# Laying the low products of a weight unit one for one between the high products of the next

## The chip, the cores and the metric

The kernel runs on one core of a Trainium2 chip. The metric is the time of one execution on the device in microseconds (us). Five engines work side by side, each through its own list of instructions in order, and wait for one another by semaphores: TensorE (PE; its weight loads are shown apart as PEld), VectorE (DVE), ScalarE (ACT), GpSimd (POOL, unused here) and SyncE (SP), which issues the transfers from memory.

## The reference

Two layers over 256 latent tokens of width 2048, with 256 context tokens that feed the first layer. All in fp32. Nearly all of the arithmetic is products of the tokens with large weight matrices:

```python
def reference(...):
    for i in range(DEPTH):                                   # 2 layers
        mod = (c_act @ mod_w[i] + mod_b[i])[:, None, :]
        sh1, sc1, g1, sh2, sc2, g2 = jnp.split(mod, N_MOD, axis=-1)
        h_lat = modulate(rms_norm(x, norm_mix_g[i]), sh1, sc1)
...
        if is_attn:                                          # layer 0
            y_lat, y_ctx = attention_mixer(h_lat, h_ctx, ...)
        else:                                                # layer 1
            y_lat = hyena_mixer(h_lat, ...)
        x = x + g1 * y_lat
        x = x + g2 * sq_relu_mlp(modulate(rms_norm(x, norm_mlp_g[i]), sh2, sc2), mlp_w1[i], mlp_w2[i])
    return rms_norm(x, final_g)
```

`sq_relu_mlp(h, w1, w2)` is `square(relu(h @ w1)) @ w2` with w1 2048 x 8192 and w2 8192 x 2048, so the two MLPs hold most of the weights.

## The kernel before

**Splitting.** To keep fp32 accuracy with a rounded matmul format (fp32r), each operand is a sum of a high part (rounded) and a low part (what the rounding left). Weights arrive in *units* of 512 x 256 values: `raw[:, n % 4]`, a ring of four slots. ScalarE copies the unit to the high part (`act_split`, writes `w_hi`), VectorE subtracts it from the raw values to get the low part (`dve_split`, writes `w_lo`); both rings have four slots too. The tokens lie as `lat` or `alt`, 512 columns per block of 128 features: 256 columns of high parts, then 256 of low parts.

**The products of a unit** (`pe_unit`). For each of 4 blocks of features (`kk`) and 2 halves of 128 output columns (`fb`) there is a *high product* (line 371: the weights' high part against all 512 columns) and a *low product* (line 380: the weights' low part against the 256 columns of high tokens, added to the same PSUM bank). The 8 high products of a unit come first, then its 8 low products. In the key projection the context tokens go along, which makes 16 and 16. In the value projection (`pe_values`, lines 408 and 415) tokens and weights change roles, and high and low products both stream 512 columns.

**Groups of units.** Eight units make a group (`pe_iter`): units 0 to 3 run through all 16 feature blocks for output columns in banks 0 and 1, units 4 to 7 for those in banks 2 and 3. A group has a number T; the MLP of each layer has 32 of them, in four quarters, each with 4 groups of the first product (tokens in `lat`) and 4 of the second (tokens in `alt`). In the attention layer, 32 units are woven between the steps of the softmax by a table, and the first group of Hyena's output projection has an order of its own; both call `pe_unit` directly. In the Hyena layer `before(n)` puts products of the convolution ahead of unit n.

**Who waits for whom.** TensorE waits for `hi_ready` (the copy) before the high products of a unit, for `split_ready` (the subtraction) before its low products, for the tokens (`ready`), and for `psum_free` before units 0 and 4. Its last low product of a unit signals `units_done`. ScalarE's copy into a slot waits for the unit's landing and for `units_done` of the unit that used the slot four units ago; VectorE's subtraction waits for the copy alone. SyncE issues the transfer of unit n + 4 when unit n is subtracted (`split_ready`), and between those, in the same list, the *slabs* of the modulation weights, which VectorE multiplies and adds up behind its subtractions. The read-outs of the PSUM banks (`act_head`, `dve_head` and their tails) stand in the lists of ScalarE and VectorE behind certain splits, and wait for `units_done` too.

Of the kernel before, what the change touches and what calls it, by code (L numbers as in the profile page):

```python
# [25 lines left out]
P = 128  # L26
# [101 lines left out]
def build(nc, a):  # L128
# [9 lines left out]
    with stack:  # L138
# [92 lines left out]
        unit_landed = [sem(f"unit_landed{j}") for j in range(RING)]  # L231
        slab_landed = [sem(f"slab_landed{j}") for j in range(RING)]
        hi_ready, split_ready = sem("hi_ready"), sem("split_ready")
        units_done = sem("units_done")
        lo_copied, psum_free = sem("lo_copied"), sem("psum_free")
        slabs_used, acc_ready = sem("slabs_used"), sem("acc_ready")
        start_landed = [sem(f"start_landed{j}") for j in range(START_RING)]
# [117 lines left out]
        def pe_unit(e, T, n, g, j, tile, ready=None, ctx_tile=None):  # L355

            e.wait_ge(hi_ready, 8 * T + n + 1)
            if ready:

                e.wait_ge(ready[0], ready[1])  # L360
            if j == 0:

                e.wait_ge(psum_free, 2 * T + g - 1)
            for kk in range(UNIT_KB):
                kb = j * UNIT_KB + kk
                if ready and len(ready) == 3 and kk == 2:
                    e.wait_ge(ready[0], ready[2])
                for fb in range(2):
                    for t, bank in ((tile, 2 * g + fb), (ctx_tile, 4 + 2 * g + fb)):
                        if t is not None:  # L370
                            e.matmul(ps[:, bank, :], w_hi[:, n % RING, kk, fb * P:(fb + 1) * P], t[:, kb, :],  # L371
                                     start=(kb == 0), stop=False)

            e.wait_ge(split_ready, 8 * T + n + 1)
            for kk in range(UNIT_KB):
                kb = j * UNIT_KB + kk
                for fb in range(2):
                    for t, bank in ((tile, 2 * g + fb), (ctx_tile, 4 + 2 * g + fb)):
                        if t is not None:
                            mm = e.matmul(ps[:, bank, 0:TOK], w_lo[:, n % RING, kk, fb * P:(fb + 1) * P],  # L380
                                          t[:, kb, 0:TOK], start=False, stop=(kb == KB - 1))
            mm.then_inc(units_done, 1)

        def pe_iter(e, T, tile, ready, ctx_tile=None, stats=None, before=None):

            for n in range(8):
                if before:
                    before(n)
                if stats is not None and n == 7:
                    pe_stats(e, *stats)  # L390
                pe_unit(e, T, n, n // 4, n % 4, tile, ready(n % 4), ctx_tile)

        V_BANKS = (0, 1, 4, 5)

        def pe_values(e, T, after_unit):

            for n in range(8):
# [5 lines left out]
                for kk in range(2):  # L403
                    kb = 2 * n + kk
                    for part in range(2):
                        for tb, bank in enumerate(V_BANKS):
                            act = (lat, alt)[tb // 2][:, kb, ds(part * TOK + tb % 2 * P, P)]
                            e.matmul(ps[:, bank, :], act, hi[:, kk, :], start=(kb == 0 and part == 0), stop=False)

                e.wait_ge(split_ready, 8 * T + n + 1)  # L410
                for kk in range(2):
# [36 lines left out]
        def act_split(e, T, n):  # L448
            e.wait_ge(unit_landed[n % RING], 16 * (2 * T + n // 4 - 1))

            e.wait_ge(units_done, 8 * T + n - 3)
            e.activation(w_hi[:, n % RING], raw[:, n % RING], ACT.Copy).then_inc(hi_ready, 1)  # L452

        def dve_split(e, T, n):
            e.wait_ge(hi_ready, 8 * T + n + 1)
            e.tensor_tensor(w_lo[:, n % RING], raw[:, n % RING], w_hi[:, n % RING].bitcast(F32),  # L456
                            ALU.subtract).then_inc(split_ready, 1)

# [656 lines left out]
        @block.tensor  # L1115
        def _(e):
            e.sem_inc(units_done, 8)
            e.sem_inc(taps_mm, 4)

            e.sem_inc(mod_cols, 1)  # L1120
# [950 lines left out]
```

## Time and profile before

| | us |
|---|---|
| median of the runs | 2599.7 |
| lowest and highest run | 2599.48, 2600.33 |
| span of the profiled execution | 2601.3 |
| TensorE, matmuls busy | 2461.9 (95%) |
| TensorE, weight loads busy | 2070.6 (80%) |
| VectorE busy | 1951.6 (75%) |
| ScalarE busy | 1170.5 (45%) |

The profile is one execution, and the span runs from its first to its last instruction. A row of the timeline has the start of an instruction, or of a row of like instructions behind one another, and the time from the start of the first to the end of the last. Matmuls overlap: a row's time is longer than the distance to the next row's start, so paces are read from starts. The mean granted TensorE clock is 0.971 of full speed over the span.

### The profile page before, as it was taken

How to read it: one execution, taken by the hardware profiler on the slowest of the kernel's cores; microseconds unless marked ns; L12 is line 12 of the kernel's file. 1: busy time of each engine (PE TensorE's matmuls, PEld its weight loads, DVE VectorE, ACT ScalarE, POOL GpSimd, SP SyncE). 2: the span in 40 equal slices, each digit the busy share in tenths (PEclk: the TensorE clock that was granted, in tenths of full speed). 3: DMA queues.
4: the chain of work that ended last, by engine and by line, in shares of the span. 5: the costliest groups of instructions: out<-in, count | busy, mean ns of one | idle time of the engine just before them, and what ended most of it. 6: DMA issues, size and time to landing. Idle time of an engine off the chain costs nothing.

```text
span 2601.3 us, 39595 instructions
## 1 busy us (share of the span) xinstructions
PE 2461.9 (95%) x13332; PEld 2070.6 (80%) x13332; DVE 1951.6 (75%) x2352; ACT 1170.5 (45%) x1611; POOL 0.2 (0%) x4
## 2 busy tenths in 40 slices
PE   6879998888999999999998999999899999999998
PEld 2248876777788888888887888888778888888887
DVE  6767777688988877877888889878786565555665
ACT  2235256535444444444446444434534444444444
POOL 0000000000000000000000000000000000000000
PEclk9989998898999999999998999999899999999999
DMA  8856865476988888888786655647696665665653
GB/s 311 299 205 229 290 189 180 150 272 236 323 307 276 289 283 281 278 273 278 270 273 236 235 197 194 235 162 239 213 341 212 189 187 187 188 190 185 188 189 124
DMA packets 441211, 610.37 MB, mean 235 GB/s; under 512 B 18875, under 2 KB 383644, under 8 KB 439068
## 3 DMA queue, kind: packets, MB, share of 16 engines
q1 hardware_dynamic: 439676, 599.98, 69.3%
q10 hardware_dynamic: 1440, 9.18, 1.0%
q8 instruction: 54, 0.88, 0.1%
q14 instruction: 41, 0.34, 0.0%
HBM read 596.50 MB, written 10.49 MB: 233 GB/s over the span
## 4 chain that ended last, share of the span: by engine, by line
PE 75%; DVE 9%; ACT 6%; issue 5%; DMA 5%; SPq 1%; DVEq 0%; ACTq 0%
PE ps L371 43%; PE ps L380 22%; DMA raw<-in_mlp_w 3%; PE ps L1139 2%; DVE w_lo L456 2%; PE ps L1371 2%; DVE acc L468 2%; ACT w_hi L452 2%; ACT hm L900 1%; PE ps L1361 1%; DVE sm L1803 1%; DMA raw<-in_attn_w_out 1%; PE ps L1156 1%; PE ps L442 1%; PE ps L1175 1%
## 5 line engine op out<-in xcount | busy, mean ns | idle before, releaser
L452 ACT ACTIVATE w_hi<-raw 128x1024 fp32r<-128x1024 f32 x720 | 761.5, 1060 | 1088.1 <-PE ps L380 857.9
L456 DVE TENSOR_TENSOR w_lo<-raw,w_hi 128x1024 fp32r<-128x1024 f32 x720 | 877.8, 1223 | 465.6 <-ACT w_hi L452 462.0
L371 PE MATMUL ps<-lat,w_hi 128*128 128x512 f32 x3136 | 817.3, 400 | 35.8 <-ACT w_hi L452 16.4
L371 PEld LDWEIGHTS ps<-lat,w_hi 128*128 128x128 f32 x3136 | 572.3, 191 | 148.4 <-issue 33.4
L371 PE MATMUL ps<-alt,w_hi 128*128 128x512 f32 x2624 | 675.0, 396 | 10.4 <-DVE alt L1790 6.2
L371 PEld LDWEIGHTS ps<-alt,w_hi 128*128 128x128 f32 x2624 | 476.0, 190 | 97.5 <-issue 6.6
L380 PEld LDWEIGHTS ps<-lat,w_lo 128*128 128x128 f32 x3136 | 433.7, 191 | 31.8 <-DVE w_lo L456 0.4
L380 PE MATMUL ps<-lat,w_lo 128*128 128x256 f32 x3136 | 446.1, 283 | 0.0
L380 PEld LDWEIGHTS ps<-alt,w_lo 128*128 128x128 f32 x2624 | 362.6, 191 | 28.4 <-DVE w_lo L456 2.7
L468 DVE SCALAR_TENSOR_TENSOR acc<-slab,silu,acc 128x1024 f32<-128x1024 f32 x300 | 378.6, 1279 | 8.0 <-DMA slab<-in_mod_w 7.0
L380 PE MATMUL ps<-alt,w_lo 128*128 128x256 f32 x2624 | 373.7, 283 | 1.9 <-DVE w_lo L456 1.9
L588 DVE SCALAR_TENSOR_TENSOR x<-ps,mod,x 128x256 f32 (+1 forms) x160 | 69.6, 476 | 18.7 <-ACT lo_sum L578 18.3
L1427 ACT ACTIVATE spec<-ps 128x512 f32<-128x512 f32 x32 | 18.1, 590 | 112.4 <-PE ps L1175 112.4
L578 ACT ACTIVATE lo_sum<-ps,mod 128x256 f32<-128x256 f32 x144 | 59.1, 461 | 12.2 <-PE ps L380 12.2
L1371 PE MATMUL ps<-back,y_spec 128*128 128x256 f32 x256 | 57.7, 379 | 0.0
L593 DVE TENSOR_TENSOR x<-x,lo_sum 128x512 f32 (+1 forms) x80 | 55.4, 692 | 2.8
L1488 ACT ACTIVATE probs<-ps,sm,rs_q 128x512 f32<-128x512 f32 x32 | 24.9, 778 | 62.3 <-DVE sm L1806 62.3
L1371 PEld LDWEIGHTS ps<-back,y_spec 128*128 128x128 f32 x256 | 47.5, 190 | 5.9
L1139 PE MATMUL ps<-slab,silu 128*2 128x512 f32 x64 | 37.9, 724 | 12.2 <-DVE start_part L1716 8.5
L612 DVE SCALAR_TENSOR_TENSOR sum_sb<-sum_sb 128x512 f32<-128x512 f32 x64 | 44.3, 692 | 2.2
L617 ACT ACTIVATE alt<-sum_sb 128x512 f32 (+1 forms) x64 | 40.2, 628 | 10.0 <-DVE sum_sb L612 10.0
L610 DVE TENSOR_TENSOR sum_sb<-ps,lo_sum 128x512 f32<-128x512 f32 x64 | 43.7, 684 | 0.4
(191 smaller groups left out, 1495.5 us busy)
## 6 DMA issues: line engine op xcount, KB each, us to landing
raw<-in_mlp_w SPq DMA_DIRECT2D x512, 512.0 KB, 3.8
slab<-in_mod_w SPq DMA_DIRECT2D x352, 512.0 KB, 6.0
raw<-in_hy_w_in SPq DMA_DIRECT2D x96, 512.0 KB, 4.4
raw<-in_attn_w_in SPq DMA_DIRECT2D x48, 512.0 KB, 4.6
raw<-in_mod_w SPq DMA_DIRECT2D x32, 512.0 KB, 6.9
raw<-in_attn_w_out SPq DMA_DIRECT2D x32, 512.0 KB, 4.6
raw<-in_hy_w_out SPq DMA_DIRECT2D x32, 512.0 KB, 5.8
spec_dram<-spec ACTq DMA_DIRECT2D x8, 1024.0 KB, 7.3
```

The source lines that it names most:

```text
L371: e.matmul(ps[:, bank, :], w_hi[:, n % RING, kk, fb * P:(fb + 1) * P], t[:, kb, :], start=(kb == 0), stop=False)
L380: mm = e.matmul(ps[:, bank, 0:TOK], w_lo[:, n % RING, kk, fb * P:(fb + 1) * P], t[:, kb, 0:TOK], start=False, stop=(kb == KB - 1))
L452: e.activation(w_hi[:, n % RING], raw[:, n % RING], ACT.Copy).then_inc(hi_ready, 1)
L456: e.tensor_tensor(w_lo[:, n % RING], raw[:, n % RING], w_hi[:, n % RING].bitcast(F32), ALU.subtract).then_inc(split_ready, 1)
L468: e.scalar_tensor_tensor(acc[:, ac], slab[:, slot], scale, acc[:, ac], ALU.mult, ALU.add).then_inc(slabs_used, 1)
L578: ins = e.activation(lo_sum[:, g, fb], ps[:, 2 * g + fb, TOK:2 * TOK], ACT.Identity, bias=bias, scale=mod[:, ds(self.gate + f, 1)])
L588: ins = e.scalar_tensor_tensor(xf, ps[:, 2 * g + fb:2 * g + fb + 1, 0:TOK], mod[:, ds(self.gate + f, 1)], xf, ALU.mult, ALU.add)
L593: e.tensor_tensor(xg, xg, lo_sum[:, g], ALU.add).then_inc(psum_free, 1)
L610: e.tensor_tensor(sum_sb[:, g], self.bank(g, 0), lo_sum[:, g], ALU.add).then_inc(psum_free, 1)
L612: e.scalar_tensor_tensor(sum_sb[:, g], sum_sb[:, g], 0.0, sum_sb[:, g], ALU.max, ALU.mult).then_inc(squared, 1)
L1139: mm = e.matmul(ps[0:2, 4 + b, :], pair, start_slot(j)[:, b * 512:(b + 1) * 512], start=(r == 0), stop=(r == len(PE_SLABS) - 1))
L1371: mm = e.matmul(ps[:, 4 + 2 * hf, fb * TOK:(fb + 1) * TOK], y_spec[:, hf, f, fb * P:(fb + 1) * P], back[:, f, :], start=(f == 0), stop=(f ...
```

## The change

The order inside a group changes (`pe_iter`). It now runs over nine blocks: block 0 holds the 8 high products of unit 0, block n the high products of unit n with the low products of unit n - 1 between them, one for one, and block 8 the low products of unit 7. A high product and the low product behind it add to the same bank (except in block 4, where the banks change). All waits of a block stand at its head, apart from that for the second half of the tokens. `pe_unit` and `pe_values` keep their order.

There are two signals now: `hi_done` from the last high product of a unit, `units_done` from its last low product. ScalarE's copy waits for `hi_done` of the unit four before; VectorE's subtraction, which overwrites the low part, waits for `units_done` of that unit in addition to the copy.

```diff
--- before.py
+++ after.py
@@ -231,7 +231,7 @@
         unit_landed = [sem(f"unit_landed{j}") for j in range(RING)]
         slab_landed = [sem(f"slab_landed{j}") for j in range(RING)]
         hi_ready, split_ready = sem("hi_ready"), sem("split_ready")
-        units_done = sem("units_done")
+        units_done, hi_done = sem("units_done"), sem("hi_done")
         lo_copied, psum_free = sem("lo_copied"), sem("psum_free")
         slabs_used, acc_ready = sem("slabs_used"), sem("acc_ready")
         start_landed = [sem(f"start_landed{j}") for j in range(START_RING)]
@@ -368,8 +368,9 @@
                 for fb in range(2):
                     for t, bank in ((tile, 2 * g + fb), (ctx_tile, 4 + 2 * g + fb)):
                         if t is not None:
-                            e.matmul(ps[:, bank, :], w_hi[:, n % RING, kk, fb * P:(fb + 1) * P], t[:, kb, :],
-                                     start=(kb == 0), stop=False)
+                            mm = e.matmul(ps[:, bank, :], w_hi[:, n % RING, kk, fb * P:(fb + 1) * P], t[:, kb, :],
+                                          start=(kb == 0), stop=False)
+            mm.then_inc(hi_done, 1)
 
             e.wait_ge(split_ready, 8 * T + n + 1)
             for kk in range(UNIT_KB):
@@ -381,14 +382,52 @@
                                           t[:, kb, 0:TOK], start=False, stop=(kb == KB - 1))
             mm.then_inc(units_done, 1)
 
+        def pe_high(e, n, kk, fb, tile, ctx_tile):
+            kb = n % 4 * UNIT_KB + kk
+            for t, bank in ((tile, n // 4 * 2 + fb), (ctx_tile, 4 + n // 4 * 2 + fb)):
+                if t is not None:
+                    mm = e.matmul(ps[:, bank, :], w_hi[:, n % RING, kk, fb * P:(fb + 1) * P], t[:, kb, :],
+                                  start=(kb == 0), stop=False)
+            return mm
+
+        def pe_low(e, n, kk, fb, tile, ctx_tile):
+            kb = n % 4 * UNIT_KB + kk
+            for t, bank in ((tile, n // 4 * 2 + fb), (ctx_tile, 4 + n // 4 * 2 + fb)):
+                if t is not None:
+                    mm = e.matmul(ps[:, bank, 0:TOK], w_lo[:, n % RING, kk, fb * P:(fb + 1) * P], t[:, kb, 0:TOK],
+                                  start=False, stop=(kb == KB - 1))
+            return mm
+
         def pe_iter(e, T, tile, ready, ctx_tile=None, stats=None, before=None):
 
-            for n in range(8):
-                if before:
-                    before(n)
-                if stats is not None and n == 7:
-                    pe_stats(e, *stats)
-                pe_unit(e, T, n, n // 4, n % 4, tile, ready(n % 4), ctx_tile)
+
+            for n in range(9):
+                if n < 8:
+                    if before:
+                        before(n)
+                    if stats is not None and n == 7:
+                        pe_stats(e, *stats)
+                    ready_n = ready(n % 4)
+                    e.wait_ge(hi_ready, 8 * T + n + 1)
+                    e.wait_ge(ready_n[0], ready_n[1])
+                    if n % 4 == 0:
+
+                        e.wait_ge(psum_free, 2 * T + n // 4 - 1)
+                if n > 0:
+
+                    e.wait_ge(split_ready, 8 * T + n)
+                for kk in range(UNIT_KB):
+                    if n < 8 and kk == 2 and len(ready_n) == 3:
+                        e.wait_ge(ready_n[0], ready_n[2])
+                    for fb in range(2):
+                        if n < 8:
+                            hi = pe_high(e, n, kk, fb, tile, ctx_tile)
+                        if n > 0:
+                            lo = pe_low(e, n - 1, kk, fb, tile, ctx_tile)
+                if n < 8:
+                    hi.then_inc(hi_done, 1)
+                if n > 0:
+                    lo.then_inc(units_done, 1)
 
         V_BANKS = (0, 1, 4, 5)
 
@@ -405,7 +444,8 @@
                     for part in range(2):
                         for tb, bank in enumerate(V_BANKS):
                             act = (lat, alt)[tb // 2][:, kb, ds(part * TOK + tb % 2 * P, P)]
-                            e.matmul(ps[:, bank, :], act, hi[:, kk, :], start=(kb == 0 and part == 0), stop=False)
+                            mm = e.matmul(ps[:, bank, :], act, hi[:, kk, :], start=(kb == 0 and part == 0), stop=False)
+                mm.then_inc(hi_done, 1)
 
                 e.wait_ge(split_ready, 8 * T + n + 1)
                 for kk in range(2):
@@ -448,11 +488,13 @@
         def act_split(e, T, n):
             e.wait_ge(unit_landed[n % RING], 16 * (2 * T + n // 4 - 1))
 
-            e.wait_ge(units_done, 8 * T + n - 3)
+            e.wait_ge(hi_done, 8 * T + n - 3)
             e.activation(w_hi[:, n % RING], raw[:, n % RING], ACT.Copy).then_inc(hi_ready, 1)
 
         def dve_split(e, T, n):
             e.wait_ge(hi_ready, 8 * T + n + 1)
+
+            e.wait_ge(units_done, 8 * T + n - 3)
             e.tensor_tensor(w_lo[:, n % RING], raw[:, n % RING], w_hi[:, n % RING].bitcast(F32),
                             ALU.subtract).then_inc(split_ready, 1)
 
@@ -1115,6 +1157,7 @@
         @block.tensor
         def _(e):
             e.sem_inc(units_done, 8)
+            e.sem_inc(hi_done, 8)
             e.sem_inc(taps_mm, 4)
 
             e.sem_inc(mod_cols, 1)
```

On TensorE, in the loop over the last groups of the second MLP (`w_hi`, `w_lo` the weights' parts, `alt` the tokens, `ps` the banks), unit 7 stood so before, as every unit did:

```order
L357 REGISTER_ALU
L371 MATMUL ps<-alt,w_hi 128x512 [waits hidden_ready,hi_ready]
L371 MATMUL ps<-alt,w_hi 128x512 x7
L380 MATMUL ps<-alt,w_lo 128x256 [waits split_ready]
L380 MATMUL ps<-alt,w_lo 128x256 x7
```

The same loop now, its blocks 0 and 1 (the pairs of a block go on to eight):

```order
L415 ISA [waits hidden_ready,hi_ready]
L389 MATMUL ps<-alt,w_hi 128x512 [waits psum_free]
L389 MATMUL ps<-alt,w_hi 128x512 x7
L411 REGISTER_ALU
L389 MATMUL ps<-alt,w_hi 128x512 [waits split_ready,hidden_ready,hi_ready]
L397 MATMUL ps<-alt,w_lo 128x256
L389 MATMUL ps<-alt,w_hi 128x512
```

The low products have moved one unit back, and the wait for the subtraction stands ahead of the next unit's first high product.

On VectorE, in the last of these groups, the last subtraction and the read-out of the first two banks behind it stood so:

```order
L456 TENSOR_TENSOR w_lo<-raw,w_hi 128x1024 [waits hi_ready]
L584 ISA
L588 ISA [waits lo_copied]
L588 REGISTER_ALU
L588 SCALAR_TENSOR_TENSOR x<-ps,mod,x 128x256
```

and now:

```order
L498 TENSOR_TENSOR w_lo<-raw,w_hi 128x1024 [waits units_done,hi_ready]
L626 ISA
L630 ISA [waits lo_copied]
L630 REGISTER_ALU
L630 SCALAR_TENSOR_TENSOR x<-ps,mod,x 128x256
```

Nothing moved there; the subtraction waits for TensorE's low products itself.

## Rows read from the trace of the kernel before

**Rows 1.** Page: TensorE's busy time, and its granted clock in 40 slices.
```profile
PE 2461.9 (95%) x13332; PEld 2070.6 (80%) x13332; DVE 1951.6 (75%) x2352; ACT 1170.5 (45%) x1611; POOL 0.2 (0%) x4
...
PEclk9989998898999999999998999999899999999999
```

**Rows 2.** Page: the chain that ended last, by engine.
```profile
PE 75%; DVE 9%; ACT 6%; issue 5%; DMA 5%; SPq 1%; DVEq 0%; ACTq 0%
```

**Rows 3.** Stages: window, length, busy time by engine, clock, DMA share, GB/s.
```profile
600.00:700.00 100.00, 89.40 (x474) 77.77 (x473) 84.89 (x98) 47.51 (x66) 0.00 (x0) 0.90 0.80 277
...
1000.00:1100.00 100.00, 100.00 (x582) 88.24 (x581) 79.14 (x79) 45.87 (x52) 0.00 (x0) 1.00 0.82 275
...
1900.00:2000.00 100.00, 92.64 (x526) 80.30 (x527) 81.08 (x84) 43.93 (x52) 0.00 (x0) 1.00 0.84 277
```

**Rows 4.** Waits from 628 to 740 us: who for whom, us, times, longest.
```profile
ACT w_hi L452 <- DMA raw<-in_mlp_w: 48.9, 20, 8.5
...
PE ps L371 <- ACT w_hi L452: 7.4, 9, 1.2
```

**Rows 5.** Page, groups: high and low products with `lat`; busy, mean ns | idle.
```profile
L371 PE MATMUL ps<-lat,w_hi 128*128 128x512 f32 x3136 | 817.3, 400 | 35.8 <-ACT w_hi L452 16.4
...
L380 PE MATMUL ps<-lat,w_lo 128*128 128x256 f32 x3136 | 446.1, 283 | 0.0
```

**Rows 6.** Timeline (start us, us, engine, ..., idle before, releaser), ScalarE, first MLP.
```profile
1003.33 1.06 ACT L452 ACTIVATE w_hi<-raw 128x1024 fp32r<-128x1024 f32 x1 [1.73 <-PE ps L380]
```

**Rows 7.** Timeline of TensorE, second MLP, first and last units of a stretch.
```profile
1969.55 2.00 PE L371 MATMUL ps<-alt,w_hi 128*128 128x512 f32 x8
1971.39 1.11 PE L380 MATMUL ps<-alt,w_lo 128*128 128x256 f32 x8
1972.34 2.00 PE L371 MATMUL ps<-alt,w_hi 128*128 128x512 f32 x8
...
2533.80 2.00 PE L371 MATMUL ps<-alt,w_hi 128*128 128x512 f32 x8
```

**Rows 8.** Timeline of TensorE, key projection: single products of 16 and 16.
```profile
226.59 0.40 PE L371 MATMUL ps<-lat,w_hi 128*128 128x512 f32 x1
...
227.75 0.39 PE L371 MATMUL ps<-alt,w_hi 128*128 128x512 f32 x1
...
228.44 0.39 PE L371 MATMUL ps<-lat,w_hi 128*128 128x512 f32 x1
...
230.25 0.28 PE L380 MATMUL ps<-lat,w_lo 128*128 128x256 f32 x1
230.36 0.28 PE L380 MATMUL ps<-alt,w_lo 128*128 128x256 f32 x1
...
231.20 0.28 PE L380 MATMUL ps<-lat,w_lo 128*128 128x256 f32 x1
...
232.16 0.40 PE L371 MATMUL ps<-lat,w_hi 128*128 128x512 f32 x1
...
259.99 0.40 PE L371 MATMUL ps<-lat,w_hi 128*128 128x512 f32 x1
```

**Rows 9.** Timeline of TensorE, value projection: 24 rows of two lie between.
```profile
290.95 0.62 PE L408 MATMUL ps<-w_hi,lat 128*128 128x512 f32 x2
...
301.83 0.39 PE L408 MATMUL ps<-w_hi,lat 128*128 128x512 f32 x1
```

**Rows 10.** Timeline of TensorE, Hyena: an inverse transform and the unit behind it.
```profile
1451.50 3.62 PE L1371 MATMUL ps<-back,y_spec 128*128 128x256 f32 x16
1454.77 2.20 PE L371 MATMUL ps<-lat,w_hi 128*128 128x512 f32 x8
```

**Rows 11.** Page: transfers of MLP weights, KB each, median us to landing.
```profile
raw<-in_mlp_w SPq DMA_DIRECT2D x512, 512.0 KB, 3.8
```

**Rows 12.** Timeline, start of Hyena: fourth unit's highs, last piece of tokens.
```profile
1391.12 2.16 PE L371 MATMUL ps<-lat,w_hi 128*128 128x512 f32 x8
...
1391.33 0.69 DVE L889 TENSOR_TENSOR lat<-hm,lat 128x512 fp32r<-128x512 f32 x1 [0.95 <-ACT lat L903]
```

## Prediction, made before the changed kernel was run

> **What bounds the kernel now.** I read the page's busy shares first. TensorE's matmul row is busy 95% of the span and its granted clock is full in most slices; DVE is at 75%, ACT at 45% [rows 1]. A busy matmul row is not proof of a bound, so the next view is the chain that ended last: 75% of it is TensorE [rows 2]. Then the stages: in the long middle of the MLPs TensorE is busy 100.00 of 100.00 us, in the first quarter of each MLP only some 89 to 93 [rows 3]. There, from 628 to 740 us, ScalarE waits 48.9 us for weights that have not landed, and TensorE for ScalarE [rows 4]. So over most of the span the time is the sum of the products on TensorE, and the change is worth what it does to their pace.
>
> The large waits of ScalarE and VectorE (ScalarE's copy after TensorE's low product, 1.73 us before a copy [rows 6]) are waits of engines with time to spare: these engines work three units ahead. Ending that wait sooner buys nothing by itself.
>
> **The pace of a unit, taken apart.** The duration of one matmul on the page (400 ns high, 283 ns low [rows 5]) overlaps its neighbours, so I use starts. An undisturbed stretch of the second MLP holds 202 units between 1969.55 and 2533.80 [rows 7]: 564.25 / 202 = 2.793 us for 8 high and 8 low products, one run after the other: 1.84 us highs, 0.95 us lows.
>
> The key projection is the same code with 16 and 16, since context tokens go along. Six of its units take 259.99 - 226.59 = 33.40 us [rows 8], 5.567 each. The 8 highs and 8 lows more cost 5.567 - 2.793 = 2.774 us, so **346.7 ns per pair** inside runs. What is left, 2.793 - 2.774 = **0.02 us, is paid once per unit**, for going from lows to highs and back.
>
> The value projection, whose high and low products all stream 512 columns, splits the pair: 48 products from 290.95 to 301.83 are 226.7 ns each [rows 9], and its turns from high to low weights cost nothing visible. So a high is 226.7 and a low 346.7 - 226.7 = 120 ns (the key projection says the same: 8 lows from 231.20 to 232.16 [rows 8]). Half the columns of a high should stream in 113.3 ns (an estimate, half of 226.7). The 6.7 ns between is most simply the next weight load, which a short product does not quite cover. It also shows where the 0.02 us sits: the first five highs after the lows take 227.75 - 226.59 = 1.16 us, 232 each, the second eight 1.81 us, 226 each [rows 8].
>
> Against this a rule can be weighed. The Trainium skill, TensorE: Matmul & The Clock Gate, LDWEIGHTS, puts a load of 128 columns at 107 ns, and its section Back-to-back issue gap puts 256 columns at about 109 ns. By the page no load is exposed in a run of lows, the unit would be 2.60 us in either order, and the change would be worth nothing. The rows disagree on the size (120 against 109), but the order-independence is a rival below.
>
> **The change, part by part.** *The order of products.* Nothing is removed: a group of 8 units has the same 64 highs and 64 lows. Now highs of unit 0 stand alone, seven blocks hold eight high-low pairs each, and lows of unit 7 stand alone. 84 groups run through the loop changed; 40 units of the attention weave and of the first Hyena output group, and the 8 value units, keep their order. In 8 of the 84 groups (first quarter of each MLP [rows 3]) arrival of data sets the pace, so I count none of their blocks: 76 x 7 = 532 blocks.
>
> What is a pair worth? While a low streams, the load for the high behind it must be done, and that load is as long as the one for a low. Nothing longer stands over it than before, so I leave the low at its 120 ns and the high at 226.7: 8 x 346.7 = 2.773 us per block, 0.020 less than now, because there is no run of lows after which the highs have to find their pace. 532 x 0.020 = **-10.6 us**. The bounds: every load covered, 8 x (226.7 + 113.3) = 2.720, -0.073 per block, -38.8 us (for it speaks that the first low behind a high starts its successor after 0.11, not 0.12 us [rows 8]); or the slow start of highs paid in each pair, +12 us and more, priced as a rival. I take the middle, because both of its terms are steady values of long runs and neither bound is.
>
> *Consecutive products on one bank.* High and low of a pair now add to the same PSUM bank, where neighbours were on two banks. No row isolates that. The inverse transform already adds four products in a row at one address: its 16 records take 1454.77 - 1451.50 = 3.27 us up to the next unit [rows 10], 204 ns each, fewer than the 226.7 of a high that alternates banks. I take 0; a cost would come on every pair, as in the slower rival.
>
> *Separate signals.* ScalarE's copy may start after the high run, 0.95 us sooner: no gain, it was early already. VectorE's split now waits for the low products itself. It used to start a copy (1.06 us) after them; now it starts with them, but they end with the following unit's highs, 1.84 us later: net 0.78 us later. Queued behind that wait on VectorE are the read-outs and modulation slabs; SyncE's next transfer of raw weights waits for the split, and the slab transfers stand behind it in its queue. The transfer is still issued about six blocks minus the split, 6 x 2.77 - 1.22 = 15.4 us, before its high product. Landing takes 3.8 us [rows 11] and the copy 1.06, so it is covered: 0. Without cover, in the 8 starved groups, it is at most 0.78 us a group, 6 us in all.
>
> *Starts of stages.* Lows of unit n now wait for unit n+1. Where the normalised tokens arrive in pieces, TensorE could do lows in the gap and no longer can. At the Hyena start the fourth unit takes 2.16 us instead of 2.00 for its highs, since its second half waits for a piece at 1391.33 + 0.69 [rows 12]; the block now wants it up to 0.95 us sooner. Four such starts at 0.5 us (half of that 0.95): +2 us; from 0 to 4. Ends of stages: the last lows stand alone as before, 0.
>
> Sum: -10.6 + 0 + 0 + 2 = -8.6 us. The profiled execution's span is 2601.3 us, 1.6 us (0.06%) over the median of the runs, 2599.7, so terms carry over unscaled: 2599.7 - 8.6 = **2591.1 us**, 0.33% faster.
>
> **Rivals.**
> - *Loads hidden for good.* If a low behind a high always streams at 113.3 and the high keeps 226.7, the pair is 340.0: 2599.7 - 38.8 + 2 = 2562.9. For it: the 0.11 us above. Against: only the first low of a run shows it, so it may be a lead built up over a run of highs and spent at once. DMA would allow it: share 0.82 in the middle of the first MLP [rows 3], 0.84 at that pace.
> - *The order does not matter* (the page's rule, worked from the rows): the 0.02 us of a block is kept in some other form, pairs stay at 349.2. Then only the stage starts count: 2599.7 + 2 = 2601.7.
> - *Slower: the turn from low to high is paid in every pair.* Place: the high behind each low. Now it is paid once in eight pairs, 2.5 ns per pair; the change loses as soon as a turn costs more than that in each pair, and loses over 0.2% from some 3.3 ns. If highs never leave the pace of their first five, the pair is 232 + 120 = 352 ns, block 2.816, +0.023: 532 x 0.023 = 12.2, so 2599.7 + 12.2 + 2 = 2613.9. If the whole 0.02 us comes with each turn, the block is 8 x 366.7 = 2.934, +74.7 us: 2676.4. Rows speak for the former, as the slow start is spread over five highs; against both, value units show no cost of changing weights.
> - *Freeing later starves the loads:* +6 us as above on top of any case; small chance by itself.
>
> **How the numbers follow.** Chances: forecast 0.32, loads hidden 0.22, no change of pace 0.16, turn paid in every pair 0.27 (0.16 near 2614, 0.11 from 2625 up), late loads 0.03. A comparison of this kernel can tell about 0.2% (5.2 us) from no change. Faster by more: loads hidden 0.22, the forecast but for the part where the starts and late loads eat it (0.26): 0.48. Within: 0.16 + 0.06 = 0.22. Slower: 0.27 + 0.03 = 0.30. The range takes in the hidden loads with starts at 0 (2561) and the slow-highs case with late loads (2620), and leaves out the full price of turns: 2560 to 2620. Both signs lie in it; the forecast's own range is 2588 to 2598.
>
> **What would show it.** In the profile after, an undisturbed stretch of the second MLP gives the pace: a block of 2.773 us, or 2.720, 2.793, 2.816, 2.93 for the rivals in turn. Starts of products inside a block should lie 227 and 120 ns apart. ScalarE's wait should name the high product's line, VectorE's split should wait on TensorE and SyncE's issues come later, with TensorE still busy 100 of 100 us there. First quarters of the MLPs should keep their length. TensorE waiting for the copy or split inside a middle stretch would make the zeros for the signals wrong; a block off 2.773 by more than 0.01 us makes the main term wrong.

## The result: slower by 0.38%

The changed kernel takes 2609.0 us (median; 2607.5 to 2614.2) against 2599.7 us of the kernel before: ratio 1.0038, 95% interval 1.0026 to 1.0049. Forecast were 2591.1 us. The time lies in the stated range, on the side of the slower rival (2613.9).

The page of the changed kernel: busy times, the chain by engine, then groups (high products, ScalarE's copy, VectorE's subtraction) with busy time, mean ns of one | idle before, what ended most of it. Line 389 of the changed kernel is the high product in the loop, 397 the low one, 492 the copy, 498 the subtraction.

```profile
PE 2471.3 (95%) x13332; PEld 2059.6 (79%) x13332; DVE 1949.1 (75%) x2352; ACT 1177.1 (45%) x1611; POOL 0.2 (0%) x4
...
PE 76%; DVE 9%; ACT 5%; issue 5%; DMA 4%; SPq 1%; DVEq 0%; ACTq 0%
...
L498 DVE TENSOR_TENSOR w_lo<-raw,w_hi 128x1024 fp32r<-128x1024 f32 x720 | 872.8, 1223 | 480.9 <-PE ps L397 411.7
L492 ACT ACTIVATE w_hi<-raw 128x1024 fp32r<-128x1024 f32 x720 | 760.2, 1059 | 909.9 <-PE ps L389 629.7
L389 PE MATMUL ps<-lat,w_hi 128*128 128x512 f32 x2944 | 1017.2, 403 | 31.2 <-ACT w_hi L492 14.2
```

Busy shares and chain are those of before [rows 1, 2] within one point; they don't show the loss. The windows do (columns as in [rows 3]):

```profile
600.00:700.00 100.00, 89.48 (x482) 76.58 (x482) 87.96 (x101) 49.36 (x69) 0.00 (x0) 0.91 0.82 282
...
1000.00:1100.00 100.00, 100.00 (x575) 87.18 (x574) 79.31 (x82) 46.89 (x53) 0.00 (x0) 1.00 0.83 284
...
1900.00:2000.00 100.00, 94.50 (x533) 80.48 (x532) 80.00 (x83) 44.74 (x52) 0.00 (x0) 1.00 0.81 273
```

From 1000 to 1100 us TensorE is busy for the whole window at the full clock, in both kernels, and gets through 575 products instead of 582 [rows 3]. So the products themselves stand farther apart. The timeline of TensorE inside a block of pairs, second MLP, shows where:

```profile
2100.03 0.40 PE L389 MATMUL ps<-lat,w_hi 128*128 128x512 f32 x1
2100.28 0.28 PE L397 MATMUL ps<-lat,w_lo 128*128 128x256 f32 x1
2100.40 0.40 PE L389 MATMUL ps<-lat,w_hi 128*128 128x512 f32 x1
2100.63 0.28 PE L397 MATMUL ps<-lat,w_lo 128*128 128x256 f32 x1
2100.74 0.40 PE L389 MATMUL ps<-lat,w_hi 128*128 128x512 f32 x1
2100.98 0.28 PE L397 MATMUL ps<-lat,w_lo 128*128 128x256 f32 x1
2101.09 0.40 PE L389 MATMUL ps<-lat,w_hi 128*128 128x512 f32 x1
```

Three pairs from 2100.03 to 2101.09 are 353 ns each. The trace's starts, to the nanosecond, repeat every three pairs: highs of 241, 236 and 233 ns, lows of 120, 113 and 117. No high comes near the 226.7 of a long run, and no low is slower than its 120. The three pairs lose 20 ns against 3 x 346.7, or 6.6 ns a pair.

A measure for whole stretches: 128 units (16 groups) of the second MLP, by the starts of the first high product of its second and of its last quarter. Before, then after:

```profile
2047.76 1.09 PE L371 MATMUL ps<-lat,w_hi 128*128 128x512 f32 x4
...
2405.30 0.86 PE L371 MATMUL ps<-lat,w_hi 128*128 128x512 f32 x3
```

```profile
2047.08 1.77 PE L389 MATMUL ps<-lat,w_hi 128*128 128x512 f32 x7
...
2408.15 1.09 PE L389 MATMUL ps<-lat,w_hi 128*128 128x512 f32 x4
```

Before, it is 357.54 us, or 2.793 us a unit as in the prediction; after, 361.07 us. The 3.53 us more lie in 16 x 7 = 112 blocks: **+0.0315 us a block**, 3.9 ns a pair, 353.1 instead of 349.2. The two longest waits from 2060 to 2400 us (who for whom: us, times, longest) are those that the prediction named:

```profile
ACT w_hi L492 <- PE ps L389: 142.5, 97, 1.8
DVE w_lo L498 <- PE ps L397: 141.7, 99, 2.0
```

ScalarE waits for the highs, VectorE for the lows; TensorE waits for nothing in this stretch.

**Where the time went, by stage.** Lengths in us, from the timelines' starts of each stage's first high product, one profiled execution each; the last two columns are experiments below.

| stage | before | after | signals alone | order alone |
|---|---|---|---|---|
| queries and keys | 75.7 | 76.7 | 76.1 | 76.3 |
| values | 55.2 | 53.5 | 53.4 | 54.3 |
| attention weave | 219.1 | 215.4 | 215.2 | 219.4 |
| attention's output | 88.5 | 90.5 | 89.5 | 90.9 |
| first MLP, first quarter's first product | 107.4 | 103.3 | 104.5 | 104.6 |
| first MLP, rest | 645.2 | 652.6 | 646.3 | 653.8 |
| Hyena, with first output group | 388.7 | 389.0 | 388.7 | 389.2 |
| Hyena's other output groups | 84.7 | 83.3 | 82.4 | 82.7 |
| second MLP, first quarter's first product | 103.1 | 102.7 | 104.1 | 102.9 |
| second MLP, rest | 643.9 | 650.7 | 643.7 | 652.5 |

Two opposite things happened: about +7 us in each MLP's long stretch, and gains in stages where TensorE has to wait. The columns of before and after differ by 6.2 us, and by 1.8 us less with the start of the program, 4.4 us. The medians differ by 9.3, because the profiled execution of before is longer than its median run and that of after the shortest of its runs: single stages with waits vary by a microsecond or two between executions, the long stretches by less. (Two executions of one kernel, the runs of 2 below, have 215.1 and 216.7 us in the weave, 104.3 and 105.5 in the first MLP's first quarter, 644.9 and 645.1 in the rest of it.)

### The profile page after: what moved, and what is told of

Same layout as the page of the kernel before. It is cut to its first block, busy times and chain, and to the rows that moved or that the text cites. A ratio compares the mean times of both kernels' runs of the same rounds, so it can differ in the third digit from the quotient of the medians.

```text
span 2605.7 us, 40388 instructions
## 1 busy us (share of the span) xinstructions
PE 2471.3 (95%) x13332; PEld 2059.6 (79%) x13332; DVE 1949.1 (75%) x2352; ACT 1177.1 (45%) x1611; POOL 0.2 (0%) x4
## 4 chain that ended last, share of the span: by engine, by line
PE 76%; DVE 9%; ACT 5%; issue 5%; DMA 4%; SPq 1%; DVEq 0%; ACTq 0%
PE ps L389 43%; PE ps L397 22%; DMA raw<-in_mlp_w 2%; PE ps L1182 2%; PE ps L1414 2%; DVE w_lo L498 2%; DVE acc L510 2%; ACT w_hi L492 2%; PE ps L1404 1%; PE ps L371 1%; DVE sm L1846 1%; DMA raw<-in_attn_w_out 1%; ACT hm L942 1%; PE ps L1218 1%; PE ps L1199 1%
## 5 line engine op out<-in xcount | busy, mean ns | idle before, releaser
L389 PE MATMUL ps<-lat,w_hi 128*128 128x512 f32 x2944 | 1017.2, 403 | 31.2 <-ACT w_hi L492 14.2
L389 PE MATMUL ps<-alt,w_hi 128*128 128x512 f32 x2496 | 851.5, 399 | 6.8 <-ACT w_hi L492 4.4
L397 PE MATMUL ps<-lat,w_lo 128*128 128x256 f32 x2944 | 767.2, 281 | 0.0
L389 PEld LDWEIGHTS ps<-lat,w_hi 128*128 128x128 f32 x2944 | 555.5, 190 | 169.2 <-issue 28.1
L397 PE MATMUL ps<-alt,w_lo 128*128 128x256 f32 x2496 | 651.4, 281 | 0.0
L389 PEld LDWEIGHTS ps<-alt,w_hi 128*128 128x128 f32 x2496 | 467.1, 188 | 117.5 <-ACT w_hi L492 7.3
L397 PEld LDWEIGHTS ps<-lat,w_lo 128*128 128x128 f32 x2944 | 534.5, 189 | 6.5
L397 PEld LDWEIGHTS ps<-alt,w_lo 128*128 128x128 f32 x2496 | 453.0, 189 | 5.6
L550 ACT ACTIVATE lo_sum<-ps 128x512 f32<-128x512 f32 x64 | 38.1, 595 | 45.8 <-PE ps L397 44.9
L371 PE MATMUL ps<-lat,w_hi 128*128 128x512 f32 x192 | 55.6, 435 | 0.9 <-DVE v L604 0.9
L689 ACT ACTIVATE u<-sum_sb,vecs 128x256 f32<-128x256 f32 x48 | 26.3, 596 | 53.4 <-DVE sum_sb L683 53.4
```

Source lines behind the costliest of these rows:

```text
L371: mm = e.matmul(ps[:, bank, :], w_hi[:, n % RING, kk, fb * P:(fb + 1) * P], t[:, kb, :], start=(kb == 0), stop=False)
L389: mm = e.matmul(ps[:, bank, :], w_hi[:, n % RING, kk, fb * P:(fb + 1) * P], t[:, kb, :], start=(kb == 0), stop=False)
```

## Experiments

**1. The two parts by themselves.** Signals alone: the order of before, with the two signals of the change.

```diff
 def act_split(e, T, n):
...
-            e.wait_ge(units_done, 8 * T + n - 3)
+            e.wait_ge(hi_done, 8 * T + n - 3)
...
 def dve_split(e, T, n):
...
+            e.wait_ge(units_done, 8 * T + n - 3)
```

> The order of products as before (8 highs, then 8 lows of a unit); only the separate signals for high and low slots stay. Theory A: the interleaved order costs about 0.032 us in each of some 560 to 588 blocks, 18 us in all, and the signals give some 9 us back, where TensorE waits for a copy (attention weave, starved groups): about 2591 us here, a unit of the second MLP at 2.793 us as before. Rival: the signals do nothing by themselves, and what was given back came from the order (work for TensorE to do while it waits): 2600 us.

Order alone: the changed kernel, with the copy waiting for `units_done` again and the subtraction for the copy only.

> The interleaved order, with one signal: the copy waits for the low products of the unit four before, as before the change. Theory A (the signals give 9 us back): about 2618 us, 0.7% slower than before. Rival (the order itself gives it back): 2609 us, as with both. Pace in the second MLP 2.825 us per block under both.

Measured: signals alone 2594.2 us, ratio to before 0.9981 (0.9972 to 0.9990); order alone 2619.3 us, 1.0086 (1.0071 to 1.0100). So the order costs 21 to 22 us by itself, and the rival by which it does not matter (2601.7 us) is out. The signals, worth nothing in the prediction, are worth 4 to 5 us in the old order and 10 to 12 in the new one (by the medians and by the ratios). The 128 units confirm the split: 357.55 us with signals alone (2040.76 to 2398.31), 361.97 with the order alone (2055.30 to 2417.27). Of the 0.90 us between this and the changed kernel, nearly all are two pauses of 0.44 us by the starts, where TensorE waits for tokens in `alt`; otherwise the blocks have the same pace. Where signals alone gain on the kernel before is in the table: values, weave, first quarter of the first MLP, Hyena's output. The gain in the last two is not shown to be the signals' own: order alone is as short there (104.6 and 82.7 us). In three of these stages ScalarE had waited for low products; the waits before, in weave, first quarter and Hyena's output (320 to 540, 628 to 736, 1766 to 1852 us), then TensorE's own from 318 to 540:

```profile
ACT w_hi L452 <- PE ps L380: 33.1, 6, 10.6
...
ACT w_hi L452 <- PE ps L380: 6.7, 3, 2.7
...
ACT w_hi L452 <- PE ps L380: 15.0, 11, 2.2
...
PE ps L371 <- DVE v L562: 2.6, 1, 2.6
```

With signals alone the second and third of these are gone from their stages, and the other two lines, both of the weave, became:

```profile
ACT w_hi L470 <- PE ps L371: 27.6, 6, 9.7
...
PE ps L371 <- DVE v L582: 0.8, 1, 0.8
```

The copy (1.06 us) now runs beside the lows (0.95 us), so the subtraction starts about when they end and not a copy later; what stands behind subtractions in VectorE's list comes sooner. One piece is plain: the read-out `v`, for which TensorE waits ahead of the weave, costs it 0.8 us instead of 2.6. Another is that TensorE's granted clock differs in places. Here are windows at about the same two places of the program, the first behind the wait for `v`, the second around a wait of 1.9 us in both kernels; before, then with signals alone:

```profile
324.00:328.00 4.00, 4.00 (x16) 3.15 (x15) 0.56 (x1) 1.70 (x2) 0.00 (x0) 0.68 0.14 58
...
732.00:737.00 5.00, 4.46 (x21) 4.31 (x22) 5.00 (x6) 4.13 (x6) 0.00 (x0) 0.66 0.77 234
```

```profile
323.00:327.00 4.00, 4.00 (x20) 3.13 (x19) 2.43 (x5) 2.39 (x3) 0.00 (x0) 0.94 0.16 58
...
726.00:731.00 5.00, 3.72 (x25) 3.37 (x26) 5.00 (x6) 4.35 (x6) 0.00 (x0) 1.00 0.76 249
```

A granted clock of 0.68 instead of 0.94 over 4 us (1 is the level of 2.4 GHz, 0.5 that of 1.2) is 1 us of work at full speed. How much of this belongs to the signals, and how much to the execution that was profiled, one profile can't tell. But the weave took 219.1 and 219.4 us in the two kernels with one signal, and 214.7 to 216.7 in all kernels with two signals and unchanged products. Which wait of the weave passes the rest of its gain on was not separated.

**2. Is it the weights in turn, the bank, or the lengths?** Three edits of the changed kernel, all one for one. The first two change what is computed and were run once each, so only the starts in their traces count, in stretches at the full clock. Low products of 512 columns (they add the weights' low part against the tokens' low part, which is not part of the kernel):

```diff
-    mm = e.matmul(ps[:, bank, 0:TOK], w_lo[...], t[:, kb, 0:TOK],
+    mm = e.matmul(ps[:, bank, 0:2 * TOK], w_lo[...], t[:, kb, 0:2 * TOK],
```

> The changed kernel with low products that stream all 512 columns instead of 256 (they add the product of the two low parts, which the original leaves out), still one for one between the highs. Theory length: only the change of length unsettles the products; equal ones run at 226.7 ns each although weights, slots and signals alternate: pair 453.3 ns, block 3.627 us in the second MLP. Rival: what unsettles them is the alternation itself (two weight tiles, two products on one bank in a row): pair 460 ns or more, block 3.68 us or more.

```profile
2103.95 0.39 PE L397 MATMUL ps<-alt,w_lo 128*128 128x512 f32 x1
2104.18 0.39 PE L389 MATMUL ps<-alt,w_hi 128*128 128x512 f32 x1
2104.41 0.39 PE L397 MATMUL ps<-alt,w_lo 128*128 128x512 f32 x1
...
2107.35 0.39 PE L389 MATMUL ps<-alt,w_hi 128*128 128x512 f32 x1
```

15 products in 3.40 us, 226.7 ns each, the pace of a long run of highs; total 3125.6 us. Weights from two rings in turn and two products on one bank cost nothing here. High products of 256 columns, too, but for those of the first block of features (the weights' high part against the tokens' low part is left out):

```diff
+    cols = 2 * TOK if kb == 0 else TOK
-    mm = e.matmul(ps[:, bank, :], w_hi[...], t[:, kb, :],
+    mm = e.matmul(ps[:, bank, 0:cols], w_hi[...], t[:, kb, 0:cols],
```

> The changed kernel, one for one, with the high products cut to 256 columns too, except those of the first feature block of each group half (left out: the weights' high part against the tokens' low part). The wide lows, where both lengths were 512, ran at exactly 226.7 ns each; but there every weight load had 226.7 ns to hide in. Here both are short and loads have only about 120 ns. Theory uneven length: two products of one length behind one another settle, whichever weights they take; 120 ns each, as in a run of lows, 240 a pair. Theory exposed load: taking weights from two places in turn lengthens the load that a short product does not cover; more than 120 each, about (353.2 - 226.7) = 126.5 or above. The loads of weights from memory then set the time (2.1 us of products per unit), so the total, somewhere from 2200 to 2500, decides nothing; starts inside a block do.

```profile
1003.94 0.29 PE L390 MATMUL ps<-lat,w_hi 128*128 128x256 f32 x1
1004.06 0.28 PE L398 MATMUL ps<-lat,w_lo 128*128 128x256 f32 x1
1004.18 0.28 PE L390 MATMUL ps<-lat,w_hi 128*128 128x256 f32 x1
...
1005.50 1.25 PE L398 MATMUL ps<-lat,w_lo 128*128 128x256 f32 x9
```

13 products in 1.56 us, 120 ns each, as in a run of lows; total 2298.6 us. So with one length throughout, long or short, alternating is free. Last, each low taken from the other half of the output columns:

```diff
-    lo = pe_low(e, n - 1, kk, fb, tile, ctx_tile)
+    lo = pe_low(e, n - 1, kk, 1 - fb, tile, ctx_tile)
```

> The changed kernel, one for one, but each low product is taken from the other half of the output columns, so that a high and the low behind it add to different PSUM banks, and each low and the high behind it to the same one. If two products on the same bank behind one another cost something only where a high comes first, the pair falls from 353.2 to about 349 ns and the time to some 2592 to 2595; in runs of 2 the neighbours lie on two banks as well, so this would also say why those are better. If the bank does not matter (the wide lows, one for one on one bank, ran at exactly 226.7 ns each), the pair stays at 353 and the time at 2607 to 2614.

2610.9 us, 1.0048 (1.0033 to 1.0062); the 128 units take 361.07 us (2048.08 to 2409.15), as in the changed kernel to the hundredth. The bank plays no part. Of the differences named in the question, the change of length is left.

**3. Does a wider low heal it?** By the prediction a low of 256 columns takes 120 ns, and not 113.3, because the next weight load is not quite covered. If that load, some 120 ns long, were also what slows the highs, a low of 320 or 272 columns would cover it. These kernels, too, compute something else and were run once each. Signals alone, with 320 columns in all low products of `pe_unit` (64 columns of the tokens' low parts go along, which is not part of the kernel), and the same in one-for-one order:

> Separate signals, runs of 8 as before the change, low products 320 columns wide instead of 256 (for 64 of the tokens they add the product of the two low parts, which the original leaves out). 320 columns at the pace of 512 (226.7) are 141.7 ns, longer than the 120 ns that a low takes now. Theory load: lows of 256 columns are held up by the next weight load, and the highs behind them have to make up for it; wide lows are not held up: 8 x (226.7 + 141.7) = 2.947 us per unit, first highs at 227 like the rest. Theory length: any change of length unsettles the highs: 2.947 + 0.02 = 2.967 us, first five highs near 232.

> The changed kernel (one for one) with the same 320-column lows. Theory load: 226.7 + 141.7 = 368.3 ns per pair, nothing lost. Theory length: about 6.5 ns lost in each pair as with 256 columns (353.2 against 346.7): 375 ns.

```profile
2205.09 2.00 PE L371 MATMUL ps<-lat,w_hi 128*128 128x512 f32 x8
2206.93 1.33 PE L381 MATMUL ps<-lat,w_lo 128*128 128x320 f32 x8
2208.09 2.00 PE L371 MATMUL ps<-lat,w_hi 128*128 128x512 f32 x8
```

Runs of 8 (2714.1 us): 1.84 us of highs, just as behind lows of 256 columns [rows 7], so the slow start is still there; single starts read 231, 236, 228, 233, 231 and then 227 ns. Lows settle at 147 ns (146.7). One for one (2739.1 us):

```profile
2203.21 0.40 PE L389 MATMUL ps<-lat,w_hi 128*128 128x512 f32 x1
2203.45 0.31 PE L397 MATMUL ps<-lat,w_lo 128*128 128x320 f32 x1
...
2207.01 0.40 PE L389 MATMUL ps<-lat,w_hi 128*128 128x512 f32 x1
```

Ten pairs in 3.80 us: 380 ns, 234 for the high and 146 for the low, 6.6 more than 226.7 + 146.7 = 373.4, the same loss as with lows of 256 columns. So a load of some 120 ns is not the cause: highs stay as slow behind a low that has 27 ns more to cover it. It does not explain the lows' own pace either. A low of 320 columns, with time to spare, would take 141.7 ns by the pace of 512; it takes 146.7, and that lies on the line through the two other lengths: (226.7 - 120) / 256 = 0.417 ns a column, and 120 + 64 x 0.417 = 146.7.

A longer load is not excluded. Its records are 0.19 us long in both orders and at every length, longer than a low of 320 columns; here that for a high behind such a low, then one of the highs of 256 columns:

```profile
2203.45 0.19 PEld L389 LDWEIGHTS ps<-lat,w_hi 128*128 128x128 f32 x1
```

```profile
1004.07 0.19 PEld L390 LDWEIGHTS ps<-lat,w_hi 128*128 128x128 f32 x1
```

In the second, products follow at 120 ns all the same, so such a load costs nothing by itself between equal products. Whether it does where a long product comes behind a short one would take two unequal lengths that both last over 0.19 us; no run has them in one number format. The nearest is Hyena's inverse transform in the kernel before [rows 10], products of 256 columns in plain fp32, whose starts lie 216 ns apart. Behind it, at 1454.77 us, the second to eighth high take 229, 233, 236, 224, 231, 236 and 228 ns: unsettled, though the load has had its time.

Lows of 272 columns in runs of 8 (16 columns of low parts go along):

> Separate signals, runs of 8, lows of 272 columns (16 tokens get the product of the low parts in addition). At the pace of 512 columns they are 120.4 ns, just what a low of 256 takes. Theory load: the lows cost no more than now, and the highs no longer start slowly: 8 x (226.7 + 120.4) = 2.777 us per unit, 0.016 less than 2.793; some 10 us over all units, 2585 us. Theory length: 2.777 + 0.02 = 2.797 us, time as with the signals alone, 2594 us.

```profile
2206.32 1.16 PE L381 MATMUL ps<-alt,w_lo 128*128 128x272 f32 x8
2207.32 2.01 PE L371 MATMUL ps<-alt,w_hi 128*128 128x512 f32 x8
```

2627.5 us. Highs start as slowly as before, and the lows take 1.00 us for 8, 125 ns each, uneven from 121 to 134: dearer than 256 columns, where a load that needs 120 ns would have left them at 120. This length alone is off the line above (126.7).

**4. How long must a run be?** Each block cut into runs of 2 or 4 highs and as many lows; or the highs of two units, then the lows of both. All have both signals.

```diff
-                for kk in range(UNIT_KB):
...
-                    for fb in range(2):
+                for at in range(0, 2 * UNIT_KB, 2):
+                    run = [(p // 2, p % 2) for p in range(at, at + 2)]
...
+                        for kk, fb in run:
```

Runs of 2, one execution, and then timed:

> The changed kernel with two highs, two lows, two highs in turn. Per pair, above 346.7: 6.5 ns are lost with runs of 1, 2.5 with 8, 1.25 with 16. Theory turn with a settling of five products: a run of 2 breaks it off early, so that a turn costs less than 20 ns but a pair loses 5 to 8 ns: 352 to 355 ns. Theory that each turn has its full 20 ns: 10 ns per pair, 357 ns. Theory that only the one-for-one order is bad: 349 ns.

> The changed kernel with two highs and two lows in turn instead of one and one; the separate signals stay. One look gave a span 12.1 us under that of the kernel before and a pair of 348.3 ns in the second MLP. If that holds, the order itself is worth 0.9 ns a pair over runs of 8, 532 x 8 x 0.9 = 4 us, on top of what the separate signals give in the old order (2594.2 against 2598.5): about 2590 to 2592, and a ratio near 0.997. If only the signals count and the runs of two are as good as runs of eight, 2594. If the one look was a lucky one, above 2597.

Runs of 4 and of 16:

> Four highs and four lows in turn, separate signals. Run lengths so far: 1 gives 353.2 ns a pair, 2 gives 348.3, 8 gives 349.2, 16 gives 348.0. If the price is one slow start per run of highs, spread over its first five products (233, 236, 228, 232, 231 against 226.7), a run of 4 pays 22.2 ns of it and its first low saves 6.7: (22.2 - 6.7) / 4 + 346.7 = 350.6 ns a pair, 1.4 over runs of 8, and the time is about 2594.2 + 532 x 8 x 0.0014 = 2600. If short runs of lows save more than that (in runs of 2 both lows take 113 to 119), it lies between runs of 2 and of 8, 348.3 to 349.2, and the time at 2590 to 2594.

> Separate signals, and longer runs in place of shorter ones: the highs of two units (16), then the lows of the two units (16). Theory turn: about 0.02 us is lost each time products of another length have to find their pace, so halving the turns saves 0.010 us per unit, 2.783 instead of 2.793 us, 6 to 7 us over some 670 units; with theory A's 9 us for the signals 2584 us, without them 2593. Rival: the 0.02 us belong to a unit (its waits and signals), not to a turn: 2.793 us per unit, 2591 or 2600 us.

| order | 128 units, us | ns a pair | time, us | ratio to before (95%) |
|---|---|---|---|---|
| 1 and 1 (changed kernel) | 361.07 | 353.1 | 2609.0 | 1.0038 (1.0026 to 1.0049) |
| 2 and 2 | 356.59 | 348.1 | 2594.8 | 0.9974 (0.9963 to 0.9985) |
| 4 and 4 | 358.62 | 350.4 | 2603.1 | 1.0012 (1.0003 to 1.0021) |
| 8 and 8 (signals alone) | 357.55 | 349.2 | 2594.2 | 0.9981 (0.9972 to 0.9990) |
| 16 and 16 | 356.27 | 347.9 | 2592.7 | 0.9976 (0.9967 to 0.9985) |

The pairs follow as above: the difference to 357.54, over 896 pairs (1024 for 16 and 16), added to 349.2. The single execution of 2 and 2 took 2591.0 us. The 128 units of the runs of 2, 4 and 16 lie at 2042.86 to 2399.45, 2042.23 to 2400.85 and 2036.27 to 2392.54 us. The timelines behind two of these rows, runs of 4 and then of 2:

```profile
2102.91 1.09 PE L389 MATMUL ps<-lat,w_hi 128*128 128x512 f32 x4
2103.84 0.64 PE L397 MATMUL ps<-lat,w_lo 128*128 128x256 f32 x4
2104.31 1.09 PE L389 MATMUL ps<-lat,w_hi 128*128 128x512 f32 x4
```

```profile
2103.20 0.62 PE L389 MATMUL ps<-lat,w_hi 128*128 128x512 f32 x2
2103.66 0.40 PE L397 MATMUL ps<-lat,w_lo 128*128 128x256 f32 x2
2103.89 0.63 PE L389 MATMUL ps<-lat,w_hi 128*128 128x512 f32 x2
...
2105.99 0.62 PE L389 MATMUL ps<-lat,w_hi 128*128 128x512 f32 x2
```

In runs of 4 the highs take 0.93 us, 232 ns each, the slow start of [rows 8]; lows 118. In runs of 2 a high and its neighbour take 0.46 to 0.47 us, 233 each, but both lows only 0.23, 115 each: eight pairs from 2103.20 to 2105.99 are 349 ns each. From 16 down to 4 the price is one slow start per run, shared by its pairs, and the expected 350.6 for 4 came out at 350.4. In runs of 2 the lows win back most of what the highs lose. Single pairs break the rule the other way: by position, the first high of a run loses 6.6 ns and the first low saves 6.7, which would leave 346.6; measured are 353.1.

Runs of 2, 8 or 16 with both signals are faster than the kernel before and than the changed one; in total time they are not told apart.

## Why the prediction was wrong

- **Bound by the pace of products on TensorE: right.** 100 of 100 us busy in both kernels, 582 and 575 products.
- **The unit taken apart: right in its sizes.** 226.7 and 120 ns in long runs, and 0.02 us once per turn, in the first five highs. Half as many turns saved 1.24 ns a pair (16 and 16), as 0.02 us over 16 pairs gives. Wrong was the reason for the lows' 6.7 ns over 113.3, a weight load not quite covered: lows of 320 columns, with more time for it, still take 5 ns over the pace of 512 (experiment 3).
- **The main term failed**, in the sentence "I take the middle, because both of its terms are steady values of long runs and neither bound is". A pair was priced from values that a product has only after several of its own length; one for one, no product is ever there. The block measures +0.0315 us instead of -0.020. The reason given, that there is "no run of lows after which the highs have to find their pace", had it upside down: one low is enough to unsettle the next high. The slower rival had the place (highs never leave their slow pace) and, at 352 ns a pair, nearly the size (353.1); its chance, 0.16, was too small for the one case whose rows [rows 8] showed highs right behind a change of length.
- **How many blocks pay:** 532 x 0.0315 would be +16.8. In the MLPs' long stretches 7.4 + 6.8 = 14.2 us came, where their 392 blocks would give 12.3. Hyena's 84 blocks, counted like the others, gave 0.3 us instead of 2.6. Of the missing 2.3 us, 1.5 are a shorter wait of TensorE for the read-out `x` at the end of that stage (1766 to 1852 us before, 1765 to 1851 after); the rest was not followed.

```profile
PE ps L371 <- DVE x L593: 2.2, 1, 2.2
```

```profile
PE ps L389 <- DVE x L635: 0.7, 1, 0.7
```

- **Same bank, 0: right** (the low from the other half, 361.07 us either way), but not for the reason given. The transform of [rows 10] has products of 256 columns in plain fp32, so its pace can't be set against the 226.7 ns of a high. Its starts lie 216 ns apart; the 204 comes of the last one, behind which the record of the next high starts after 29 ns.
- **Separate signals, 0: wrong**, in "no gain for ScalarE, it was early already". That was read in the long stretches [rows 6], where it holds. In the stages that wait, ScalarE's wait for lows, 33.1 + 6.7 + 15.0 us in three of them, was not priced at all; only a loss was considered there. Measured: -4 to -5 us in the old order, -10 to -12 in the new, where lows end later. Without them the miss would have been larger (2619.3 us); that the time came so near to the rival's 2613.9, which has the signals at 0 too, is in part luck.
- **Transfers of weights covered: right.** TensorE waits for nothing from 2060 to 2400 us. The first MLP's first quarter did not keep its length, it became shorter (107.4 to 103.3 us); the second's kept it (103.1 and 102.7).
- **Starts of stages, +2:** queries and keys +1.0, attention's output +2.0, but these hold the price of their pairs too, so the term was not measured by itself.

A product's pace here is no function of its own length alone: 512 columns take 226.7 ns in a run and 233 to 241 between products of 256 columns, at the full granted clock. The Trainium skill, TensorE: Matmul & The Clock Gate, section Back-to-back issue gap, gives the spacing of weight loads and products by the number of columns, 131 ns sustained for 512 and about 216 for a product by itself. This trace agrees with neither, and here it decides.

**Open:** why a change of length unsettles TensorE, why single pairs fall into a period of three, and why runs of 2 do better than runs of 4. Shown is that the loss comes with unequal lengths, and neither with weights in turn, nor with the bank, nor with a load of some 120 ns; that a load of 0.19 us plays no part behind a short product is made likely by the highs behind the transform, not shown.

## What to carry to other kernels

The steady pace of a long run of like matmuls is no price for the same matmuls taken in turn with others of another length: look in the trace for the first products behind a change, and try run lengths of 1, 2, 4 and 8, since they are not in order. Separate signals for the readers of a buffer are worth pricing in the stages that wait, not in those where the freed engine has time to spare. A change made of two parts wants each part run alone: here one part lost over 20 us and the other won 4 to 12, and their sum hid both.

## What the runs showed of the hardware

- Products of equal length taken in turn from two weight buffers run at the pace of one run: 226.7 ns at 512 columns, 120 at 256.
- Behind 8 lows of 256 or 320 columns, highs of 512 need five products to settle, behind 272 columns six (behind 256: 233, 236, 228, 232, 231 ns, then 227).
- 512 and 256 one for one settle into a period of three pairs, 353.3 ns on average; 512 and 320 into 380 ns, steady. Both are 6.6 ns a pair over the paces of long runs.
- A run of 272 columns takes 125 ns a product, unevenly; 256 columns take 120, 320 columns 146.7, 512 columns 226.7, which is 0.417 ns a column and 13.3 ns a product in all three.
